# Layer one of a macaron decoder layer: eight plain tiles and seven pairs in place of six and eight, on all PSUM banks, the first four weight units side by side

## The reference

```python
def rmsnorm(x, g):
    return x * lax.rsqrt(jnp.mean(x * x, axis=-1, keepdims=True) + 1e-6) * g

def swiglu(x, w_gate, w_up, w_down):        # w_gate, w_up: 1024 x 2816, w_down: 2816 x 1024
    return (jax.nn.silu(x @ w_gate) * (x @ w_up)) @ w_down

h = h + 0.5 * swiglu(rmsnorm(h, ffn1_norm), ffn1_w_gate, ffn1_w_up, ffn1_w_down)
h = h + mixing(rmsnorm(h, mix_norm))        # pooling and windowed attention, gated
h = h + 0.5 * swiglu(rmsnorm(h, ffn2_norm), ffn2_w_gate, ffn2_w_up, ffn2_w_down)
```

## Time and profile before

| | |
|---|---|
| median of 3 runs | 1071.86 us (1069.93 to 1073.36) |
| the profiled execution | 1071.72 us, its span 1069.9 us |
| TensorE busy | 1046.2 us, 98% of the span |
| VectorE busy | 655.3 us, 61% |
| ScalarE busy | 478.9 us, 45% |
| GpSimd busy | 435.2 us, 41% |
| mean DMA rate | 118 GB/s |

### The profile page before, as it was taken

The page is one execution under the profiler, slowest core; times in us unless marked ns, Lnnn a source line. Parts: engine busy times, 40 slices in busy tenths (PEclk is TensorE's granted clock), DMA queues, the critical chain, the costliest instruction groups (busy, mean ns, idle before and its releaser), DMA issues.

```text
span 1069.9 us, 15524 instructions
## 1 busy us (share of the span) xinstructions
PE 1046.2 (98%) x6024; PEld 912.7 (85%) x6024; DVE 655.3 (61%) x1008; ACT 478.9 (45%) x825; POOL 435.2 (41%) x240
## 2 busy tenths in 40 slices
PE   6889999999999999999999999999999999999998
PEld 5769999998888888887777788888889999988887
DVE  5899757758530178426766746668986577584101
ACT  6434555545332243336767653344345555453110
POOL 1442342335444443344545544444423423354441
PEclk9999999999999999999999999999999999999999
DMA  7434775732323342222111113306347757323332
GB/s 279 110 97 118 188 205 160 182 115 99 99 98 99 100 165 79 79 79 80 59 59 59 59 42 117 99 20 206 99 128 187 207 159 186 111 99 99 99 99 99
DMA packets 42033, 126.35 MB, mean 118 GB/s; under 512 B 4336, under 2 KB 4336, under 8 KB 41968
## 3 DMA queue, kind: packets, MB, share of 16 engines
q1 hardware_dynamic: 37216, 108.41, 30.6%
...
## 4 chain that ended last, share of the span: by engine, by line
PE 84%; DVE 10%; ACT 2%; issue 2%; DMA 1%; SPq 0%; DVEq 0%; ACTq 0%
PE psum L485 16%; PE psum L487 16%; PE psum L486 16%; PE psum L538 10%; PE psum L540 10%; PE psum L539 10%; PE psum L771 1%; DVE gate L1405 1%; DVE moving_sums_low L1440 1%; PE psum L786 1%; DVE hidden L1409 1%; PE psum L799 1%; DVE u_blocks_low L1435 1%; PE psum L800 1%; PE psum L801 1%
## 5 line engine op out<-in xcount | busy, mean ns | idle before, releaser
L1261 POOL TENSOR_TENSOR w_low_in_place<-w_raw,w_high 128x1024 fp32r<-128x1024 f32 x66 | 164.7, 2500 | 207.3 <-ACT w_high L865 207.3
L865 ACT ACTIVATE w_high<-w_raw 128x1024 fp32r<-128x1024 f32 x116 | 122.3, 1055 | 216.3 <-DMA w_raw<-weights_dram 168.7
L1261 POOL TENSOR_TENSOR w_low<-w_raw,w_high 128x1024 fp32r<-128x1024 f32 x50 | 122.9, 2461 | 109.9 <-ACT w_high L865 109.9
L485 PE MATMUL psum<-hidden_high,w_high 128*128 128x512 f32 x352 | 137.0, 389 | 0.0
L486 PE MATMUL psum<-hidden_low,w_high 128*128 128x512 f32 x352 | 136.9, 389 | 0.0
L487 PE MATMUL psum<-hidden_high,w_low_in_place 128*128 128x512 f32 x352 | 136.9, 389 | 0.0
L1371 DVE SCALAR_TENSOR_TENSOR h<-psum,h 128x512 f32<-128x512 f32 x24 | 16.5, 689 | 150.8 <-PE psum L487 150.8
L485 PE MATMUL psum<-u_high,w_high 128*128 128x512 f32 x240 | 98.1, 409 | 0.0
L485 PE MATMUL psum<-ffn_u_high,w_high 128*128 128x512 f32 x192 | 79.0, 411 | 15.3 <-DVE gate L1394 7.1
L487 PE MATMUL psum<-u_high,w_low 128*128 128x512 f32 x240 | 93.9, 391 | 0.0
L486 PE MATMUL psum<-u_low,w_high 128*128 128x512 f32 x240 | 93.7, 391 | 0.0
...
## 6 DMA issues: line engine op xcount, KB each, us to landing
w_raw<-weights_dram SPq DMA_DIRECT2D x117, 512.0 KB, 3.5
gate_a<-weights_dram SPq DMA_DIRECT2D x16, 512.0 KB, 6.2
gate_s<-weights_dram SPq DMA_DIRECT2D x16, 512.0 KB, 3.6
gate_s<-weights_dram POOLq DMA_DIRECT2D x16, 512.0 KB, 6.5
up_a<-weights_dram SPq DMA_DIRECT2D x16, 512.0 KB, 4.7
up_s<-weights_dram SPq DMA_DIRECT2D x16, 512.0 KB, 3.6
up_s<-weights_dram POOLq DMA_DIRECT2D x16, 512.0 KB, 8.6
...
```

Source lines behind the costliest of these rows:

```text
L485: pe.matmul(o, wh, xh, start=start, stop=False)
L865: act.activation(high[:, s, :], raw[:, s, :], ACT.Copy).then_inc(high_done, 1)
L1261: pool.tensor_tensor(wlow[:, s, :], raw[:, s, :], high[:, s, :], ALU.subtract).then_inc(low_done, 1)
```

## The change

`PLAIN` becomes (8, 6), so that layer one has 16 plain units and seven pairs, and layer two keeps 12 and eight. In both layers the plain tiles take turns on all eight banks (`plain_bank`); the bank of the sum of squares moves, and unit 7 waits until VectorE has read it. The wait for `gate_scaled` and `up_scaled` starts with tile 4 and asks for the tile four back.

Units 0 to 3 of layer one come as four quarters, each two units by two blocks, and then four second halves. TensorE takes a block of the activations through all four units before the next one, and in the first tile it begins with the high parts alone. GpSimd does the low parts of the second halves of units 2 and 3. Five square buffers stand in place of two.

ScalarE's and VectorE's lists between the plain tiles are written anew for both layers. The pair buffers take turns from each layer's first pair on (`buffer`, `fills`); that renames buffers and issues nothing.

```diff
-PLAIN = (6, 6)
+PLAIN = (8, 6)
+QUARTERS = ((0, 0), (2, 0), (0, 1), (2, 1))
-SUM_BANK = (0, 4, 0)
+SUM_BANK = (1, 4, 3)
+def plain_bank(n, f):
+    k = PLAIN[n] - 1 - f
+    return (0, 6, 2, 4)[k % 4] if PAIRS[n] % 2 else (4, 6, 2, 0)[k % 4]
...
@@ SyncE, start
             load_x(0)
-            sp.dma_start(raw[:, 0, 0:UNIT // 2], weights_in[0, :, 0:UNIT // 2]).then_inc(first_landed, 16)
+            load_quarter(0)
             load_x(1)
-            sp.dma_start(raw[:, 0, UNIT // 2:UNIT], weights_in[0, :, UNIT // 2:UNIT]).then_inc(raw_landed[0], 16)
-            for i in range(2, len(X_PIECES) - 1):
-                load_x(i)
-            load(1)
-            load(2)
+            load_quarter(1)
+            load_x(2)
+            load_quarter(2)
+            load_quarter(3)
+            load_x(3)
+            load_second_half(0)
+            load_x(4)
+            for u in range(1, SLOTS):
+                load_second_half(u)
             sp.dma_start(consts[:, :], consts_in).then_inc(consts_landed, 16)
-            load(3)
-            load_used(4)
-            gate_prologue(0)
-            for u in range(5, U_DN1):
+            for u in range(SLOTS, U_DN1):
                 load_used(u)
+                if u == SLOTS + 2:
+                    gate_prologue(0)
@@ TensorE, plain
+            def first_units(xh, xl):
+                first_tile(xh, xl)
+                for i, (u, part) in enumerate(QUARTERS):
+                    pe.wait_ge(quarter_low, i + 1)
+                    for c in range(2 * part, 2 * part + 2):
+                        pe.wait_ge(u_low[0], c + 1)
+                        for s in (u, u + 1):
+                            if i or c:
+                                passes(unit_bank(0, s), s, c, xh[:, c, :], xl[:, c, :], c == 0, False, raw_low)
+                for s in range(SLOTS):
+                    if s == SLOTS - 1:
+                        sum_of_squares(0)
+                    if s < 2:
+                        pe.wait_ge(quarter_low, len(QUARTERS) + 1 + s)
+                    else:
+                        pe.wait_ge(low_done, lows(s))
+                    for c in range(TILES // 2, TILES):
+                        pe.wait_ge(u_low[0], c + 1)
+                        mm = passes(unit_bank(0, s), s, c, xh[:, c, :], xl[:, c, :], False, c == TILES - 1, raw_low)
+                    mm.then_inc(unit_used, 1)
                 for f in range(2, PLAIN[n]):
                     k = f % 2
-                    pe.wait_ge(F["gate_scaled"], f - 1)
-                    project(base + 2 * f, 2 * k, 4 + 2 * k, xh, xl, wlow=raw_low)
+                    if f >= 4:
+                        pe.wait_ge(F["gate_scaled"], f - 3)
+                    project(base + 2 * f, 2 * k, unit_bank(n, 2 * f), xh, xl, wlow=raw_low)
@@ TensorE, first product of a pair's gate; and S1, which waits for the last tile as before
-                        pe.wait_ge(F["up_scaled" if k else "gate_scaled"], PLAIN[n] - 1)
+                        pe.wait_ge(F["up_scaled" if k else "gate_scaled"], PLAIN[n] - 3)
@@ VectorE, plain: the end of the list
-                plain_scaled(base, 5, F)
+                    plain_scaled(n, base, 6, F)
+                    plain_silu(6, F)
+                dve.wait_ge(unit_used, base + 2 * PLAIN[n] - 1)
                 weight_sums(g, up_w)
                 low_a1(g, up_w)
-                plain_hidden(5, F)
                 low_s2(g, up_w)
                 low_s31(g, up_w)
+                if not n:
+                    dve.wait_ge(unit_used, base + 2 * PLAIN[n])
+                    plain_product(6, F)
+                plain_tile(PLAIN[n] - 1)
```

323 lines of the change are left out of this document (220 added, 103 removed).

## The result

The changed kernel takes 1062.74 us (median of 4 runs, 1061.78 to 1063.18); the kernel before took 1071.21 (4 runs). The ratio is 0.9919, with a 95% interval of 0.9904 to 0.9933: faster by 0.8%, where 1.4% was forecast. The profiled execution has a span of 1060.7 us against 1069.9. The forecast span was 1054.4, so 6.3 us of it are missing.

What follows compares the result with a forecast made beforehand. TensorE, busy 98% of the span, was taken as the bound. Layer one's 11.7 us and layer two's 3.8 take the span from 1069.9 to 1054.4 us, so 1056 us; forecast 1053 to 1058.5, wider range 1052 to 1062.5.

Steps and rivals of the forecast that it cites:

- The start: Layer one's first units: TensorE's first matmul at about 6.0 us, full clock by 11 us, no wait for x.
- The small pieces: Start's 256 KB loads: cost 0 to 2.6 us, taken as 0; rival that they are slow, 1058.5 us, chance 0.06.
- Both gate waits: Layer one's plain stage: TensorE's two waits for gate (7.1 us) and their low clock (3.0 us) go.
- A pair: Layer one's seven pairs: 20.2 us each where nothing waits, 141.4 us together.
- Layer two's wait of 2.1 us: Layer two's first pair: the up product's 2.1 us wait goes, with 1.7 us of low clock.
- VectorE's sum: Layer one's plain stage: VectorE has 62 us of work less up to 2, through at 97.5 to 99.5 us.
- The term of 2.1 us: Layer one, before the first pair: all TensorE waits from VectorE's lateness and late low parts, 2.1 us (bounds 0 and 7).
- the prediction's own signs of being wrong: Layer one: low-part wait over 2 us in units 8 to 15, clock dip after 15 us, or four units ending after 33.
- the prediction's sum without waits: Layer one's plain stage: TensorE without any wait reaches the first pair at 96.4 us.
- Hidden by 1.2 us: Layer one's first pair: up_s load and addition with issues take 9.7 us against 10.9 to the pair, so hidden.
- I take the whole wait to go, with its low clock: 3.8 us: Layer two's first pair: the new order at the lists' end saves 3.8 us (bounds 1.2 and 3.8).
- VectorE as bound: Rival: VectorE bounds layer one's plain stage, ending at 103 to 105 us with clock dips; 1060 to 1063 us, chance 0.22.

Runs made afterwards that it cites:

- 100.34 in one run: Changed kernel with layer two's list end ordered as before the change (last tile scaled ahead of the up sums), layer one untouched: 1063.03 us, ratio 0.9921.
- 99.38 with 1.5 us less of VectorE's work: Changed kernel with GpSimd's issue of the gate's two adding loads put behind unit 8's subtraction, not unit 7's: 1059.73 us, ratio 0.9890.
- the old order on the best kernel: Kernel with all refills earlier and adding loads behind unit 8, with layer one's list end ordered as before the change: 1059.12 us, ratio 0.9890.
- the old order there: Changed kernel with layer two's list end ordered as before the change, layer one untouched: 1063.03 us, ratio 0.9921.
- the other: Trace of the changed kernel run again without any edit: 1062.88 us, ratio 0.9919.
- GpSimd's wait: Changed kernel with GpSimd waiting, in each layer's first pair, for VectorE's last plain product before the up product's late low parts: 1061.44 us, ratio 0.9893.

## Why the prediction was off

**Right.** The start: TensorE at 6.02 us, full clock at 11.28 against 11, the latter by luck, since with this start it came between 8.9 and 12.1 us in other traces. The small pieces cost nothing. By the Trainium skill (DMA: Bandwidth & Descriptors, Measured) loads below 1 MiB fall well short of the peak; its table is of loads that GpSimd issues, these are issued by SyncE. The trace disagrees again, with 400 GB/s from 10 to 15 us and no wait of TensorE for them. Both gate waits with their low clock are gone. A pair is 20.2 to 20.3 us where nothing waits. Layer two's wait of 2.1 us with its low clock is gone at its place. VectorE's sum was right too: 62 us less 2 from 37.5, forecast 97.5 to 99.5, measured 98.7, though it began 0.8 us later.

**The step that failed, first part:** "*by my walk along the lists the low parts of units 12, 13 and 15 come up to 1.5 us late each. I take 2.1 us for all of it*". VectorE's end was right, but the walk from it to the low parts was not. Unit 15's comes at 95.04 us, and TensorE without a wait wants it at 90.96: 4.1 us late and not 1.5. Unit 11, which the walk does not name, is 2.2 us late. The term of 2.1 us measured 4.3 (100.72 - 96.4), and two of the prediction's own signs of being wrong came: a wait of over 2 us for a low part (2.04) and a fall of the clock in layer one. The chain to unit 15 can be read off the profile: tile 5's scaling at 90.00 us, which is VectorE's end of 98.7 less the 8.7 us of work behind that scaling, and from there tanh, refill and subtraction, 5.0 us. What I had missed as well is where VectorE loses its time. Its lateness was averaged over the stretch, while in fact the eight blocks, which take 7.19 us in the run with one subtraction there, took 11.15 right at the front with two and the loads' issue; that is how unit 11 came to be late.

That two units bind at once is shown by the runs. With unit 11's wait short and no low clock, unit 15 still sets the first pair (100.34 in one run, 99.38 with 1.5 us less of VectorE's work). With unit 15's refill moved alone, unit 11 sets it (100.12). With unit 11's moved alone, the wait goes to unit 12 (101.20). With all refills moved it is 96.41, the 96.4 of the prediction's sum without waits, and without GpSimd's subtractions 95.56 us.

**Second part:** "*Hidden by 1.2 us*", of the load and the addition of `up_s`. It left out that the adding load stands behind unit 15's subtraction on GpSimd, and that behind tile 5's tanh. The load was issued 1.7 us later than it could be, and `up_a_low` came 0.9 us late. Shown by the run with unit 15's refill earlier.

**Third part:** the waits after the first pair's start have no term. The order of the list's end was costed by what it saves `up_a_low`, not by what stands behind the last tile now: its SiLU and product, then the first pair's additions and the second pair's weight sums. TensorE waits for these 18 us later, 1.1 us in layer one and 1.0 in layer two. That the two waits trade one for the other is shown in layer one by the old order on the best kernel, and in layer two by the old order there, with equal times. The mis-sized term is "I take the whole wait to go, with its low clock: 3.8 us": the wait went, and half of its gain came back in the one trace and all of it in the other, where the second pair's load landed a us later. Of the 3.8 only 3.3 could be had.

The rival "VectorE as bound" named 1060 to 1063 us. Its mechanism is what happened in layer one's plain stage, milder than it gave (103 to 105 us; 100.7 measured), and its size rests on GpSimd: with its subtractions gone the stage never waits. That its time was hit is in part luck, since 1.9 us were lost in layer two, of which it says nothing. The further 0.4 us of the miss are the profiled execution's distance from span to median.

**Left open.** In layer two the load of the second pair's `up_s` is issued 0.2 us after the first pair's start; why GpSimd could go on behind it after 4.0 us in some traces and 5.1 in others is not known. What GpSimd's wait is worth in the median, and what the banks bring without the new start, was not settled. The best version measured is that with all refills earlier and adding loads behind unit 8: 1058.3 us, against 1062.9 for the changed kernel on the same chip, every execution of the one below every one of the other.
